# Multiplications into an unread bank in the gaps of four norms

## What is computed

```python
# first block
x = layer_norm(ALPHA * x + hybrid_mixer(x), ln1)               # norm n1
x = layer_norm(ALPHA * x + memory_cross_attention(x, mem), ln2) # norm n2
x = layer_norm(ALPHA * x + conv_ffn(x), ln3)                    # norm n3
# second block
h = rms_norm(x, g_pre_mix) * (1 + scale1) + shift1              # folded into n3
merged = sigmoid(gl_a) * y_a + sigmoid(gl_b) * y_b + sigmoid(gl_c) * y_c   # from h @ w_in
x = x + gate1 * rms_norm(merged @ w_o, g_post_mix)              # the mixer norm
h2 = rms_norm(x, g_pre_ffn) * (1 + scale2) + shift2             # folded into the mixer norm
gt, up = split(h2 @ w_ffn_in)
x = x + gate2 * rms_norm((silu(gt) * up) @ w_ffn_out, g_post_ffn)
```

## Time and profile before

| | |
|---|---|
| median of 3 runs | 907.14 us (905.70 to 909.64) |
| profiled execution | 910.18 us |
| its span, first to last instruction | 908.4 us |
| mean granted TensorE clock | 0.967 |
| TensorE multiplications, busy | 857.2 us (94%) |
| DVE busy | 650.9 us (72%) |
| ACT busy | 503.5 us (55%) |

### The profile page before, as it was taken

The page is one execution under the profiler, slowest core; times in us unless marked ns, Lnnn a source line. Parts: engine busy times, 40 slices in busy tenths (PEclk is TensorE's granted clock), DMA queues, the critical chain, the costliest instruction groups (busy, mean ns, idle before and its releaser), DMA issues.

```text
span 908.4 us, 15935 instructions
## 1 busy us (share of the span) xinstructions
PE 857.2 (94%) x6384; PEld 812.0 (89%) x6384; DVE 650.9 (72%) x1008; ACT 503.5 (55%) x721; POOL 7.7 (1%) x17
## 2 busy tenths in 40 slices
PE   4999998989899999999997999999899899999997
PEld 4889986889798999999997889899899899999886
DVE  3675686778567888787866896777798766665553
ACT  4644447446456766655445765786658555444452
POOL 0200000000000000000000000000000000000000
PEclk8999999999997999999998999999999699999999
DMA  9784474765252666566762366456565277775661
GB/s 323 195 254 117 157 227 160 228 204 186 70 165 91 206 187 186 184 184 228 260 217 91 106 205 216 149 181 203 174 209 163 70 254 228 234 234 185 149 223 47
DMA packets 139577, 166.91 MB, mean 184 GB/s; under 512 B 5504, under 2 KB 123264, under 8 KB 139504
## 3 DMA queue, kind: packets, MB, share of 16 engines
q1 hardware_dynamic: 137712, 162.82, 57.1%
q0 software_dynamic: 720, 2.02, 0.9%
q10 hardware_dynamic: 1072, 1.05, 0.3%
HBM read 164.62 MB, written 1.25 MB: 183 GB/s over the span
## 4 chain that ended last, share of the span: by engine, by line
PE 36%; DVE 10%; ACT 6%; issue 2%; DVEq 0%; ACTq 0%
PE ps L508 36%; DVE lor L1582 4%; DVE FA L1582 2%; ACT hir L1083 2%; DVE FA L1585 1%; ACT L1421 1%; ACT X L1353 0%; ACT HIH L1359 0%; DVE raw L1599 0%; ACT FA L1421 0%; ACT FA L1463 0%; DVE INL L1582 0%; DVE FA L1588 0%; ACT FA L1363 0%; DVE FA L2235 0%
## 5 line engine op out<-in xcount | busy, mean ns | idle before, releaser
L1582 DVE TENSOR_TENSOR lor<-raw,hir 128x1024 fp32r<-128x1024 f32 (+1 forms) x266 | 309.5, 1181 | 113.1 <-ACT hir L1083 105.4
L1083 ACT ACTIVATE hir<-raw 128x1024 fp32r<-128x1024 f32 (+1 forms) x258 | 261.2, 1032 | 122.9 <-PE ps L508 109.0
L508 PE MATMUL ps<-INH,hir 128*128 128x256 f32 (+1 forms) x1064 | 309.3, 291 | 17.6 <-DVE lor L1582 13.9
L508 PE MATMUL ps<-INL,hir 128*128 128x256 f32 (+1 forms) x1064 | 305.2, 287 | 1.1 <-DVE INL L1582 0.9
L508 PE MATMUL ps<-INH,lor 128*128 128x256 f32 (+1 forms) x1064 | 304.2, 286 | 0.0
L508 PEld LDWEIGHTS ps<-INH,hir 128*128 128x128 f32 x1064 | 207.1, 195 | 21.5 <-issue 16.7
L508 PEld LDWEIGHTS ps<-INL,hir 128*128 128x128 f32 x1064 | 206.4, 194 | 2.0 <-DVE INL L1582 2.0
L508 PEld LDWEIGHTS ps<-INH,lor 128*128 128x128 f32 x1064 | 206.9, 194 | 1.0 <-issue 1.0
L508 PE MATMUL ps<-HIH,hir 128*128 128x256 f32 x688 | 200.0, 291 | 6.4 <-DVE lor L1582 4.2
L508 PE MATMUL ps<-HIH,lor 128*128 128x256 f32 x688 | 196.0, 285 | 0.0
L508 PE MATMUL ps<-HIL,hir 128*128 128x256 f32 x688 | 195.8, 285 | 0.0
(11 more groups left out here) (266 smaller groups left out, 778.9 us busy)
## 6 DMA issues: line engine op xcount, KB each, us to landing
raw<-in_w_in SPq DMA_DIRECT2D x64, 512.0 KB, 4.5
raw<-in_mod_wT SPq DMA_DIRECT2D x48, 512.0 KB, 4.3
raw<-in_ffn_w_up SPq DMA_DIRECT2D x44, 512.0 KB, 4.2
raw<-in_w_ffn_in SPq DMA_DIRECT2D x44, 512.0 KB, 4.6
raw<-in_w_ffn_out SPq DMA_DIRECT2D x22, 512.0 KB, 4.6
raw<-in_ffn_w_down SPq DMA_DIRECT2D x20, 512.0 KB, 5.0
raw<-in_xa_wkv SPq DMA_DIRECT2D x16, 512.0 KB, 4.0
raw<-in_xa_wq SPq DMA_DIRECT2D x8, 512.0 KB, 5.4
```

Of the source, the lines that this page charges most:

```text
L508: return e.matmul(o, l, r, start=start, stop=stop, skip_group_check=True)
L1083: e.activation(hi, src, ACT.Copy).then_inc(*w_hi.up(i))
L1582: return e.tensor_tensor(o, a, b, op)
```

## The change

A function `warm(name, n)` takes one more bank of `att` and issues n multiplications of `HIH` by `HIH` (128x128 by 128x256), each as a whole group, into it. Nobody reads the bank. Its name is never marked as copied, so `copied` treats it as free at once. At n1 and n2 there are 2 + 2 + 3 + 4 + 8 of them, after the third norm 40, at the mixer norm 4 + 3 + 3 + 4 + 8.

```diff
         def copied(name):
-            if name is None:
+            if name is None or name[0] == "warm":
                 return act, 0
...
+            def warm(name, n):
+                b, before = att.get(("warm", name), bank)
+                w.wait_ge(copied(before))
+                def some(n):
+                    for _ in range(n):
+                        mul(b[:, 0:T], HIH[:, 0, 0:128], HIH[:, 0, :])
+                some(n)
+                return some
...
                 t.then_inc(*mm.up((name, "early")))
+                more = warm(name, 2)
                 w.wait_ge(dve.at((name, "x", 3)))
...
+                more(2)
                 w.wait_ge(act.at((name, "sq", 3)))
...
             def layer_norm(name):
-                row_sums(name, 3, X[:, 6:8, :])
+                more = row_sums(name, 3, X[:, 6:8, :])
+                more(3)
                 spread_bank((name, "mu"), SN[:, 0:2])
+                more(4)
                 spread_bank((name, "r"), SN[:, 6:8])
+                more(8)
...
             spread(b, r3b, "n3 r2")
             run(g)
+            warm("third norm", 40)
...
+            more = warm("mixer norm", 4)
             w.wait_ge(act.at("mix q 3"))
...
+            more(3)
             w.wait_ge(dve.at("mix e 2"), dve.at("mix f 2"))
...
             t.then_inc(*mm.up("mix y"))
+            more(3)
             spread_bank("mix r", rm)
+            more(4)
             spread_bank("mix r2", rm2)
+            more(8)
```

More of the change, by code:

```diff
@@ L778, in row_sums @@
                 t.then_inc(*mm.up((name, "sums")))
+                return more
             def spread_bank(name, v):
```

## The result

The changed kernel is slower by a little: 911.07 us as the median of 19 runs (907.06 to 916.04) against 907.73 us for the kernel before in 19 runs (904.11 to 911.96), a ratio of 1.0039 with a 95% interval of 1.0024 to 1.0055. Forecast were 909.9 us from 907.14 us, +2.8 us; measured are +3.3 us from 907.73 us.

What follows compares the result with a forecast made beforehand. Behind the norms TensorE, slowed by clock dips, was taken to be only 0.18 to 0.58 us behind DVE, which feeds it. Terms 0.1 + 0.8 + 0 + 0.4 + 1.5 = +2.8 us on 907.14 gave 909.9 us, range 904.5 to 914.

Steps and rivals of the forecast that it cites:

- DVE paces the stretch behind a norm: Behind n1, n2 and mixer norm, TensorE's next unit waits for DVE's tiles; a faster TensorE wins at most 0.18, 0.58, 0.51 us.
- I expect the clock to fall about where it fell.: At n1, 11 new multiplications, 1.3 us in 4.6 us, don't prevent the clock's fall; it comes back earlier.
- the first rival: Clock stays at 2.4 GHz through the gaps: n1 -0.3, n2 -1.2, mixer -1.0, together -2.5 us, 904.6 us; chance 0.17.
- n1 +0.1: At n1, two additions between the sums cost 0.23 us, partly offset by the lag: +0.1 us (-0.3 to +1.1).
- n2 +0.8: At n2, copy 0.4 us later plus 0.9 before DVE resumes, less 0.5 of lag: +0.8 us (-1.2 to +1.3).
- Third norm 0: 40 additions take 4.7 us in a 5.74 us gap, free; unit v's faster start is lost waiting for HIL.
- `dt` +0.4: Moved bank makes dt wait 2.54 us, taken up by a later wait; possible leak booked +0.4 us (0 to +4.0).
- The rival that I gave 0.20: dt's 2.54 us wait plus a 1.5 us dip reach the end: all 4.0 us stay, 913.5 us; chance 0.20.
- Mixer norm +1.5: Additions delay the FA sums, DVE's copy and second spread; less the 0.51 us lag, +1.5 us (-1.0 to +2.0).
- lag of 0.51 us: Mixer norm: TensorE's start at 722.21 is 0.51 us behind DVE's tile at 721.70, the most a faster TensorE can win.
- likeliest case: The forecast itself, the sum of the terms at n1, n2, third norm, dt and mixer norm: 909.9 us; chance 0.50.
- the clock is kept: The first rival; at the mixer norm FA sums -0.9, paid back by 0.82, spread -0.5, plus 0.51: -1.0 us; chance 0.17.

Runs made afterwards that it cites:

- e2: Only the 22 added multiplications at the mixer norm, none elsewhere, against the kernel before: 909.22 us, ratio 1.0017 (0.9995 to 1.0038).
- e4: Only the 40 behind the third norm, with the moved bank, against the kernel before: 907.09 us, ratio 0.9992 (0.9975 to 1.0010).
- e7: Only the 4 + 3 at the mixer norm ahead of the FA sums, against the kernel before: 910.14 us, ratio 1.0032 (1.0012 to 1.0052).
- e8: Only the mixer norm's additions, all but the last 8 doubled, against the kernel before: 908.46 us, ratio 1.0016 (0.9999 to 1.0033).
- e10: Only the 3 + 4 + 8 at the mixer norm behind the FA sums, against the kernel before: 906.69 us, ratio 1.0005 (0.9988 to 1.0022).
- e11: Only the 22 at the mixer norm, timed once more, against the kernel before: 909.74 us, ratio 1.0030 (1.0011 to 1.0050).
- e1: The changed kernel with the bank of the third norm's 40 given back to the rotation; timed against the kernel before: 909.47 us, ratio 1.0021.
- e3: Only the 19 each at n1 and n2, against the kernel before: 907.92 us, ratio 1.0002 (0.9980 to 1.0025).
- e5: The changed kernel keeping only additions in idle stretches, without the moved bank; timed against the kernel before: 907.03 us, ratio 0.9986.
- e9: The changed kernel timed again in a later series, against the kernel before: 908.32 us, ratio 1.0023 (1.0003 to 1.0042).
- e12: e5 with the third norm's early column sums cut in two groups, the first moved earlier; against the kernel before: 904.99 us, ratio 0.9984.
- e6: The changed kernel with each added multiplication cut to 4 moving columns; timed against the kernel before: 912.45 us, ratio 1.0069 (1.0045 to 1.0093).

## Why the prediction was right, and where its steps were off

- **DVE paces the stretch behind a norm.** Shown at n1, and at n2 within the lag of 0.58 us that the prediction gives: at n1 TensorE had a granted clock of 1.00 over 11.6 us where it had 0.71, and n1 to n2 takes 73.55 us in place of 73.59; the waits for `INL` in the whole execution went from 0.9 to 5.2 us. That was the central step.
- **"I expect the clock to fall about where it fell."** Wrong at n1. In the profiled execution of every kernel without additions there (before, e2, e4, e7, e8, e10, e11) the clock fell at n1, either behind the copy (n1 to n2 73.6 to 73.7 us) or earlier (74.5 to 74.8 us). With additions of 256 columns it held in after, e1, e3 and e5 (73.3 to 73.6 us), and fell in e9 and e12 (74.3 and 74.6 us); with those of 4 columns (e6) it fell. Against the late fall a kept clock is worth 0.3 to 0.4 us (e5 against before and e10), since DVE paces; the changed kernel spends 0.23 of that on the two additions between the sums. Against the early fall it is worth 1.0 to 1.5 us. At n2 it fell as I said in after, e1 and e3, but e9 kept it, and there the last of the 96 products is 0.99 us earlier than in before, with all additions paid; the first rival had said 1.2 for n2. So that rival was near in its price at n2, too high at n1 (0.3 us, measured 0.04 in after), and wrong in that the clock was not kept at n2 in after, nor at the mixer norm in any execution of the changed kernel. I had read the step from the fall behind 14 dense multiplications at the third norm and from n1 itself, but the trace of before, with its idle stretches, could not tell what filling them does.
- **n1 +0.1.** Measured -0.04 in after; the mean of after, e1, e3 and e9 is 73.74 us, that of before, e2, e4, e7, e8, e10 and e11 74.08, and the scatter of 1.2 us is larger than both. With the clock kept in both, after takes 0.25 us more than e5, which lacks the two additions between the sums: their 0.23 us is there, and the kept clock covers it.
- **n2 +0.8.** After: the copy 3.75 us behind the first sum (before 3.77), where I said 0.4 later, as the clock fell about 0.5 us later behind that sum; DVE's work with `r` 7.10 us behind it (before 6.28), +0.82 where I said 1.3. To the last of the 96 products and to the third norm's sums +0.4. The mechanism is there and the net is half of the forecast, but it is the difference of +1.2 us for the additions and about -0.7 us for the clock, and comes out from -1.0 (e9) to +0.75 us (e1) behind the norm.
- **Third norm 0.** Shown by e4, within its interval of -2.3 to +0.9 us; in after as in e4 TensorE waits 1.6 us for the second tile of `HIL`, where before it waited 0.4, so what v gained by its clock is lost there, as forecast.
- **`dt` +0.4.** The idle stretch is there, 2.44 us, ended by DVE's copy, as forecast, the later wait is shorter by 1.55 us, and 0.0 of it is left at the mixer norm (after, e4, e9). The rival that I gave 0.20 happened once, in e6, for 0.7 us: there the clock fell behind the idle stretch, and the later waits for weights are gone altogether.
- **Mixer norm +1.5.** The copy +1.60 (said 1.5), the second factor +2.24 (said 1.9), at the end +1.9. Of the lag of 0.51 us, 0.35 was used up. This term is the bulk, and e2, e11 and e7 with it alone, e10 without it, show it.
- **The sum.** +2.8 forecast, +3.3 measured (2.2 to 5.0 by the interval), +2.1 by the ratio of the second series (e9: 0.3 to 3.8; its medians differ by 1.4). By the segments it is 0 + 0.4 + 0 + 1.9 = 2.3. That the first series shows 1 us more than the segments is within its interval and stays open. Part of the closeness is luck: n1, n2 and `dt` were each booked too high, 1 us together, and the mixer norm 0.4 too low. The 908.2 to 911.5 us that the prediction gives for its likeliest case doesn't follow from its own bounds either: with both small bounds, -1.2 and -1.0, the sum is 905.4 us.

What I didn't foresee is that the cost isn't proportional: at the mixer norm 7 additions ahead of the `FA` sums did not keep the clock in any of six profiled executions with 256 columns, and 14 kept it in that of e8. The rival "the clock is kept" I had priced with the sums over `FA` -0.9 and +0.82, and e8 shows that trade, with 1.6 us paid.

## What to carry to other kernels

Before buying a clock, look at what the next stretch waits for: where TensorE is only some tenths of a microsecond behind the engine that feeds it, twice the clock gives back those tenths (0.3 us at n1, 0.7 at n2) and the rest is turned into waits. Filling belongs only where an engine is idle anyway; an addition ahead of a short string of dependent work costs its issue time, and more if it pushes that string past a fall of the clock. A scratch buffer taken from a rotation moves every later one: look for new waits in the instruction list. Moving real work into an idle stretch, as e12 did, costs no instruction; its 1 us shows in the trace and is too small for these times.

## What the runs showed of the hardware

- A multiplication of 4 moving columns holds its place for as long as one of 256 at 2.4 GHz, 0.11 us against 0.11 to 0.12 (e6, after), and doesn't keep the clock as those do (mean granted clock 0.963 to 0.970 against 0.976 to 0.987).
- Column sums, one behind the other with no idle time, don't keep the clock: at the mixer norm of before TensorE was busy for all of the 3.60 us ahead of the fall.

```profile
702.20:705.80 3.60, 3.60 (x34) 1.00 0.55 181
705.90:707.52 1.62, 1.62 (x9) 0.50 0.86 268
```

- The same list keeps or loses the clock from one execution to the next: third norm to v takes 28.0, 29.5 or 31.0 us, and n1 to n2 73.6 or 74.7 us, in kernels that are alike there. With the start up to n1, 192.7 to 197.4 us, this is as much as the spread of 904 to 912 us of the kernel before, and that spread goes with the mean granted clock of its runs.
- Multiplications that nobody reads can keep the clock: with 19 at n1 it was 1.00 over 11.6 us instead of 0.71 (after; also in e1 and e3, and with 13 in e5, not in e9 and e12; in none of the seven executions without additions there). It is not certain in any one execution.
